# New orders of the pieces in the engine lists of both attentions of a two-layer hybrid encoder

## The reference

```python
def block(q_start, qn, qp):                      # MLA
    sc = (einsum('bqhd,bkhd->bhqk', qn, k_nope) + einsum('bqhr,bkr->bhqk', qp, k_pe)) * scale
    p = softmax(where(chunk_causal_mask(q_start, s), sc, neg), axis=-1)
    return einsum('bhqk,bkhd->bqhd', p, v)

def block(q_start, qb):                          # differential
    sc = einsum('bqhcd,bkhcd->bchqk', qb, k) * scale
    p = softmax(where(chunk_causal_mask(q_start, s), sc, neg), axis=-1)
    a = p[:, 0] - lam * p[:, 1]
    return einsum('bhqk,bkhd->bqhd', a, v)
# then: o = rmsnorm(o, g_subln) * (1 - lambda_init)
```

## Time and profile before

| | |
|---|---|
| median of 3 runs | 2595.37 us (2592.87 to 2596.51) |
| profiled execution, its own time | 2595.02 us |
| its span, first to last instruction | 2593.2 us |
| mean granted clock of TensorE, as a share of full speed | 0.972 |
| PE busy | 2409.5 us, 93% |
| DVE busy | 1794.5 us, 69% |
| ACT busy | 914.6 us, 35% |
| GpSimd busy | 1494.3 us, 58% |

### The profile page before, as it was taken

The page is one execution under the profiler, slowest core; times in us unless marked ns, Lnnn a source line. Parts: engine busy times, 40 slices in busy tenths (PEclk is TensorE's granted clock), DMA queues, the critical chain, the costliest instruction groups (busy, mean ns, idle before and its releaser), DMA issues.

```text
span 2593.2 us, 31553 instructions
## 1 busy us (share of the span) xinstructions
PE 2409.5 (93%) x11916; PEld 1974.8 (76%) x11916; DVE 1794.5 (69%) x2043; ACT 914.6 (35%) x1553; POOL 1494.3 (58%) x1123
## 2 busy tenths in 40 slices
PE   7899999999999999996899899978999999999993
PEld 5688888778888888883677787766778888888882
DVE  3566674797777777778666677763687777777778
ACT  3344442352222222224346565652342222222222
POOL 2222113637999999974441323213628999999982
PEclk9999999999999999997999999988999999999996
DMA  4121225311111111113121212142411111111103
GB/s 155 57 66 63 68 79 198 138 57 57 49 49 49 49 59 64 49 65 126 54 66 33 73 50 90 33 163 107 138 64 42 65 50 49 49 49 59 64 33 130
DMA packets 51237, 191.98 MB, mean 74 GB/s; under 512 B 5904, under 2 KB 6416, under 8 KB 47376
## 3 DMA queue, kind: packets, MB, share of 16 engines
q1 hardware_dynamic: 39184, 148.92, 17.0%
q10 hardware_dynamic: 11904, 41.05, 4.1%
HBM read 146.43 MB, written 29.36 MB: 68 GB/s over the span
## 4 chain that ended last, share of the span: by engine, by line
PE 74%; DVE 15%; ACT 5%; issue 3%; DMA 2%; SPq 1%; ACTq 0%; POOL 0%; POOLq 0%; DVEq 0%
PE ps L1222 9%; PE ps L1224 9%; PE ps L1223 9%; PE ps L1249 6%; PE ps L1251 6%; PE ps L1250 6%; PE ps L1058 3%; PE ps L1030 2%; PE ps L1032 2%; PE ps L1031 2%; PE ps L1095 2%; PE ps L1075 2%; PE ps L1150 1%; PE ps L1015 1%; PE ps L1151 1%
## 5 line engine op out<-in xcount | busy, mean ns | idle before, releaser
L2096 DVE TENSOR_TENSOR a<-a,ps 128x1024 f32<-128x1024 f32 x336 | 408.7, 1217 | 205.9 <-PE ps L1251 194.0
L768 POOL CAST w_hi<-w_raw 128x1024 fp32r<-128x1024 f32 x78 | 85.5, 1096 | 799.9 <-PE ps L1032 276.6
L1249 PE MATMUL ps<-hid,ring 128*128 128x512 f32 x704 | 277.5, 394 | 18.8 <-DVE a L2096 15.3
L850 POOL TENSOR_TENSOR ring<-w_raw,ring 128x512 fp32r<-128x512 f32 x206 | 268.4, 1303 | 16.5
L1250 PE MATMUL ps<-hid,ring 128*128 128x512 f32 x704 | 275.5, 391 | 0.0
L1251 PE MATMUL ps<-hid,ring 128*128 128x512 f32 x704 | 275.4, 391 | 0.0
L1599 ACT ACTIVATE cy<-cx,cv 128x1024 f32<-128x1024 f32 x76 | 94.8, 1247 | 416.7 <-DVE cx L2067 415.4
L1222 PE MATMUL ps<-h,ring 128*128 128x512 f32 x608 | 236.5, 389 | 0.0
L1223 PE MATMUL ps<-h,ring 128*128 128x512 f32 x608 | 236.5, 389 | 0.0
L1224 PE MATMUL ps<-h,ring 128*128 128x512 f32 x608 | 236.5, 389 | 0.0
L848 POOL CAST ring<-w_raw 128x512 fp32r<-128x512 f32 x206 | 128.5, 624 | 122.0 <-PE ps L1177 53.4
(11 more groups left out here) (274 smaller groups left out, 6760.6 us busy)
## 6 DMA issues: line engine op xcount, KB each, us to landing
w_raw<-in_W SPq DMA_DIRECT2D x166, 512.0 KB, 3.2
raw_d<-in_W SPq DMA_DIRECT2D x44, 512.0 KB, 3.8
h<-o_dram ACTq DMA_DIRECT2D x2, 6144.0 KB, 21.4
x_dram<-x ACTq DMA_DIRECT2D x6, 2048.0 KB, 7.2
x<-x_dram SPq DMA_DIRECT2D x2, 4096.0 KB, 12.2
dsw<-draw SPq DMA_DIRECT2D x64, 128.0 KB, 2.3
o_dram<-most SPq DMA_DIRECT2D x6, 1024.0 KB, 4.9
o_dram<-dost SPq DMA_DIRECT2D x6, 1024.0 KB, 4.4
```

Source lines behind the costliest of these rows:

```text
L850: pool.tensor_tensor(lo, raw[name], hi.bitcast(F32), ALU.subtract).then_inc(item_ready, 1)
L1249: pe.matmul(out, wh, xh, start=True, stop=False)
L2096: dve.tensor_tensor(a[:, f, :], a[:, f, :], src, ALU.add).then_inc(acc_done, 1)
```

## The change

The strings of `ORDERS` are replaced, for both attentions and for all four engines. Each new string has the same pieces as the old one, each once; only their order differs. Nothing else in the file is touched; the places, counts, banks, the last chunk that uses a buffer and `load_after` are worked out from the lists as before. Cut to the lines that are spoken of:

```diff
+++ after.py
@@ -164,112 +164,107 @@
...
 ORDERS = {
     "mla": {
         "pe": """
-            E00 E01 Q00 Q01 K00 K01 S000 V00 S001 S010 S011 V01 T000 S020 T010 V02 T011 P000 S021 V03 P010 P011
-            S030 K10 T020 T021 S031 K11 T022 P020 P021 Q10 T030 P022 T031 Q11 P030 T032 P031 K20 P032 T033 S100
-            S101 K21 P033 S110 T100 Q20 P100 S111 Q21 S120 E10 T110 T111 S121 E11 P110 P111 S130 V10 T120 T121
...
-            T232 Q31 P230 P231 T233 K40 P232 P233 S300 K41 S301 S310 S311 Q40 T300 S320 Q41 P300 T310 T311 S321
...
-            Q60 P500 S511 Q61 S520 E30 T510 S521 E31 P510 T511 S530 V30 P511 S531 T520 T521 T522 P520 P521 T530
...
-            P611 V33 S621 K70 S630 T620 K71 T621 P620 T622 S631 Q70 P621 P622 T630 T631 Q71 T632 T633 P630 P631
...
-            P721 T730 P722 T731 T732 P730 P731 T733 P732 P733""",
+            E00 E01 Q00 Q01 K00 K01 V00 S000 S001 K10 S010 S011 T000 V01 S020 P000 Q10 S021 T010 T011 V02 S030 Q11
+            T020 T021 P010 P011 V03 S031 K11 T022 P020 P021 Q20 S100 T030 T031 P022 E10 P030 T032 S101 E11 P031 T033
...
+            T122 S201 Q31 P120 P121 T130 K31 P122 S210 T131 P130 T132 V10 P131 S211 T133 V11 P132 S220 T200 V12 P133
...
+            P420 E30 P421 P422 T430 T431 E31 S510 S511 T432 T433 P430 P431 K61 P432 P433 T500 Q60 S520 Q61 P500 S521
+            S530 T510 T511 S531 Q70 S600 P510 P511 T520 T521 Q71 S601 P520 T522 P521 T530 K70 P522 S610 T531 T532
...
+            V32 S700 S701 T622 P620 P621 S710 S711 T630 P622 T631 V33 T632 T633 P630 P631 S720 T700 S721 P632 P633
+            S730 T710 P700 T711 S731 T720 P710 P711 T721 T722 P720 P721 T730 P722 T731 T732 P730 P731 T733 P732 P733""",
         "act": """
...
+            T610 T611 S621 K71 S630 S631 o61 T620 T621 V32 S700 S701 T622 T630 o62 T631 V33 S710 T632 T633 S711 S720
+            T700 o63 S721 T710 o70 T711 S730 T720 o71 T721 S731 T722 T730 o72 T731 T732 T733 o73""",
...
         "dve": """
...
+            M720 T700 o63 S721 S730 M721 T710 o70 T711 M730 S731 T720 o71 T721 M731 T722 T730 o72 T731 T732 T733 o73""",
         "sp": """
-            L2 L3 WE0 X0 L4 X1 L5 L6 L7 D0 L8 WE1 L9 X2 X3 D1 L10 L11 D2 L12 WE2 L13 X4 X5 D3 L14 L15 D4 WE3 X6
-            X7 D5""",
+            WE0 L2 L3 X0 L4 L5 X1 L6 WE1 L7 D0 L8 X2 X3 D1 L9 L10 L11 WE2 D2 X4 D3 L12 X5 L13 WE3 L14 D4 L15 X6 X7
+            D5""",
     },
...
     "diff": {
         "pe": """
...
-            K71 N61 P620 T621 T622 Q70 P621 P622 T630 T631 Q71 N62 P630 P631 T632 T633 P632 P633 N63 S700 S701
-            S710 S711 T700 P700 S720 N70 T710 T711 S721 P710 P711 N71 S730 T720 T721 P720 P721 S731 T722 P722
-            N72 T730 T731 T732 P730 T733 P731 P732 P733 N73""",
...
+            N53 S621 T610 P600 K70 S630 T611 K71 S631 N60 P610 Q70 P611 T620 T621 Q71 T622 P620 P621 T630 P622 N61
+            T631 P630 N62 S700 S701 T632 P631 T633 S710 S711 T700 P632 S720 P633 S721 T710 N63 P700 S730 T711 P710
+            N70 P711 S731 T720 T721 T722 P720 N71 P721 P722 T730 T731 T732 P730 P731 T733 P732 P733 N72 N73""",
         "act": """
...
-            M630 K70 o61 n60 S631 s60 M631 K71 n61 T621 T622 s61 rK7 Q70 o62 T630 T631 Q71 n62 s62 T632 T633 o63
-            rQ7 n63 s63 S700 S701 M700 M701 S710 T700 S711 M710 o70 M711 n70 S720 s70 T710 T711 M720 o71 S721
-            n71 M721 s71 T720 T721 S730 M730 T722 S731 o72 M731 n72 T730 T731 s72 T732 T733 o73 n73 s73""",
...
+            T630 s60 o62 n61 rQ7 s61 T631 n62 S700 S701 M700 T632 M701 S710 S711 M710 s62 T633 M711 T700 S720 o63
+            M720 T710 S721 n63 o70 M721 T711 s63 S730 o71 n70 M730 T720 T721 S731 T722 M731 s70 n71 T730 T731 o72
+            s71 T732 T733 o73 n72 n73 s72 s73""",
         "dve": """
...
-            T630 T631 Q71 n62 s62 T632 T633 RQ7 rQ7 n63 s63 S700 S701 i700 i701 M700 S710 M701 S711 T700 i710
-            i711 M710 S720 M711 n70 i720 s70 T710 T711 S721 M720 i721 n71 M721 s71 S730 T720 T721 i730 M730 S731
-            T722 i731 M731 n72 T730 T731 s72 T732 T733 n73 s73""",
...
+            T621 M630 M631 n60 Q71 s60 T622 RQ7 T630 n61 rQ7 T631 S700 S701 i700 n62 S710 i701 M700 S711 M701 T632
+            i710 i711 M710 S720 M711 T633 s61 i720 S721 s62 T700 T710 M720 i721 n63 S730 T711 M721 s63 i730 S731 n70
+            T720 M730 i731 T721 T722 M731 s70 n71 T730 T731 T732 T733 s71 n72 n73 s72 s73""",
         "sp": """
-            L2 L3 WK0 L4 WQ0 L5 L6 L7 WK1 L8 WQ1 L9 WK2 L10 WQ2 L11 D0 L12 D1 L13 WK3 L14 WQ3 L15 WK4 D2 L16 WQ4
-            L17 L18 D3 L19 WK5 L20 WQ5 L21 WK6 L22 D4 WQ6 L23 D5 WK7 WQ7 D6""",
+            L2 L3 WK0 WQ0 L4 L5 L6 WK1 L7 WQ1 L8 L9 L10 WK2 D0 WQ2 L11 D1 WK3 L12 L13 WQ3 L14 WK4 L15 WQ4 L16 D2 L17
+            WK5 L18 L19 D3 WQ5 WK6 L20 L21 D4 WQ6 L22 L23 WK7 D5 WQ7 D6""",
     },
 }
...
```

More of the change, by code:

```diff
@@ L177 @@
-            S600 S601 P522 T531 T532 S610 P530 P531 T533 S611 V31 P532 P533 T600 T610 V32 P600 T611 S620 P610
-            P611 V33 S621 K70 S630 T620 K71 T621 P620 T622 S631 Q70 P621 P622 T630 T631 Q71 T632 T633 P630 P631
-            S700 S701 P632 P633 S710 T700 S711 S720 P700 S721 T710 T711 S730 P710 P711 S731 T720 T721 T722 P720
-            P721 T730 P722 T731 T732 P730 P731 T733 P732 P733""",
-        "act": """
[L182 to L193, removed]
@@ L194 @@
-        "dve": """
[L195 to L209, removed]
@@ L215 @@
         "pe": """
[L216 to L220, removed]
@@ L226 @@
-            P511 S530 N51 V30 S531 T520 T521 P520 T522 P521 S600 S601 P522 S610 T530 N52 S611 T531 T532 P530
-            T533 P531 T600 V31 T610 S620 P532 P533 V32 S621 N53 V33 S630 T611 T620 P600 P610 K70 S631 P611 N60
-            K71 N61 P620 T621 T622 Q70 P621 P622 T630 T631 Q71 N62 P630 P631 T632 T633 P632 P633 N63 S700 S701
-            S710 S711 T700 P700 S720 N70 T710 T711 S721 P710 P711 N71 S730 T720 T721 P720 P721 S731 T722 P722
-            N72 T730 T731 T732 P730 T733 P731 P732 P733 N73""",
@@ new lines @@
+            K00 K01 Q00 Q01 V00 S000 S001 V01 S010 S011 V02 S020 T000 V03 P000 T010 S021 N00 K10 T011 S030 K11 S031
+            P010 P011 T020 Q10 P020 T021 T022 Q11 P021 N01 T030 P022 T031 K20 T032 T033 P030 P031 S100 S101 K21 S110
+            S111 P032 P033 N02 T100 S120 Q20 S121 N03 P100 T110 T111 S130 Q21 S131 P110 N10 P111 T120 T121 V10 T122
+            P120 N11 S200 S201 P121 P122 T130 T131 S210 T132 P130 P131 T133 S211 V11 T200 P132 S220 V12 S221 P133
+            V13 N12 N13 T210 P200 S230 K30 T211 N20 K31 T220 S231 P210 T221 P211 Q30 P220 T222 Q31 P221 T230 P222
@@ new lines @@
+            T231 K40 N21 P230 P231 T232 T233 S300 S301 K41 S310 S311 N22 P232 P233 T300 S320 Q40 N23 P300 S321 T310
+            T311 Q41 S330 N30 P310 P311 T320 T321 S331 V20 S400 N31 P320 T322 S401 P321 T330 S410 P322 T331 S411
+            P330 T332 P331 T333 V21 P332 T400 S420 V22 P333 S421 V23 N32 S430 N33 P400 T410 T411 K50 S431 K51 N40
+            P410 P411 T420 T421 Q50 T422 N41 P420 Q51 P421 T430 P422 T431 K60 P430 T432 P431 T433 S500 S501 K61 S510
+            S511 T500 P432 Q60 S520 P433 P500 N42 N43 S521 T510 T511 Q61 S530 P510 N50 P511 T520 S531 T521 V30 S600
```

100 lines of the change are left out of this document (59 added, 41 removed).

## The result

The changed kernel took 2575.47 us (median of 4 runs, 2571.65 to 2577.93), the kernel before beside it 2595.76 (4 runs, 2592.87 to 2596.51): a ratio of 0.9919 [0.9907, 0.9931], or 20 us less. The forecast was 40. The profiled execution took 2573.36 us.

What follows compares the result with a forecast made beforehand. TensorE was taken to bound the kernel, waiting for latency rather than throughput. MLA body 12, differential body 20 and head 7 8 summed to 40 us, so 2595 - 40 = 2555 us; range 2531 to 2584.

Steps and rivals of the forecast that it cites:

- half the gain: Rival, 2576 us: middle pieces on DVE and ACT late for other reasons; MLA 7, body 10, head 7 2; chance 0.2.
- that rival: Rival, slower, 2601 us: DVE standing at the 20 exchanges holds PE 2.3 us each, 46 against 40; chance 0.07.
- MLA body, 12: MLA attention's body: shorter waits of PE and less clock loss save 12 us, bounds 4 and 18.
- the two terms for waits: MLA body: 6 of the 8.0 us behind DVE's block tails go, and the 2.8 before one chunk.
- the term of 3 for clock and hidden pauses: MLA body: fewer pauses give back 3 us of lower-clock time and short pauses hidden in the rows.
- MLA opening, 0: Start of the MLA attention: PE's order hardly changes, so 0, between -2 and +2 us.
- Differential body, 20: Differential attention's body: shorter waits of PE, clock and hidden pauses save 20 us, bounds 6 and 32.
- The terms for P (8.5) and N (3.5): Differential body: probabilities-times-V waits shrink 6.5 behind DVE and 2 behind the previous output; norm-sum waits shrink 3.5 of 4.7.
- The terms for S and T (2.5): Differential body: waits of score pieces and transposes shrink by 2.5 us.
- Last score piece of a block to its first T: Both attentions: median PE work before the first transpose grows, MLA 6.2 to 11.2 us, differential 11.7 to 14.3.
- Head 7, 8: Last differential head: a serial score chain with two shortened links saves 8 us, bounds 0 and 16.
- The two shortened links: Head 7: one exponent no longer behind an output copy; work from last scores to their transposes grows 1.3 to 3.6 us.

Runs made afterwards that it cites:

- the doubling: All 20 exchanges of halves done twice, the second after the first landed: 2674.59 us on the changed kernel, 2710.63 us on the kernel before.
- the part that was tested: GpSimd's multiplications by the norm gains left out of the differential attention: 2564.82 us on the changed kernel, 2585.48 us on the kernel before.
- the last kernel: Changed kernel with transposed-block tails ahead of norms and rotations in all differential heads, plus the MLA opening's old nine-piece order on ACT and DVE: 2592.99 us.

## Why the prediction was half right

The measured 2575.5 us lie in the stated range, but 9 us above the favoured forecast of 2543 to 2566: the range held because it took in the rival "half the gain", which had a chance of 0.2.

- **Direction and mechanism** were right: PE waited for latency, and longer distances in its list took those waits away. P behind DVE fell to 0.5 us in the differential body (under 4 forecast) and to 0.4 in MLA (under 2). The feed-forward parts stayed equal, and the bulk load cost nothing, as worked out. The exchange did not take over the end: DVE's wait there stayed at 18.6 and 18.4 us, so that rival fell.
- **MLA body, 12:** measured 15 (311.1 to 298.9, with the 2.9 us of the opening set apart), inside the bounds of 4 and 18. The size is right, its make-up less so: 6.5 us of idle time went, not the 8.8 of the two terms for waits, and the term of 3 for clock and hidden pauses came out at 8 to 9. Of this the clock is worth up to 5.7 (283 us at 0.98, now 1.00).
- **MLA opening, 0:** it cost 2.9 us in this profile, 1.0 to 3.2 in the six kernels with these MLA lists, two of them outside the 2 allowed; the lower clock there (0.76 for 0.88) goes with it. The prediction named V00 ahead and RE0 later on DVE and priced both at nothing. That rE00 meets a split is new, but the old places on ACT and DVE don't bring the time back.
- **Splits on GpSimd, 0:** waits of PE behind a split are new, 1.4 us in each body.
- **Differential body, 20:** 7.9 us less idle time, about 10 by the windows (434 to 424). The terms for P (8.5) and N (3.5) were, if anything, small: 11.3 and 4.7. The terms for S and T (2.5) and for the chunks (2) had the wrong sign: -6.4 and -1.8. The clock term of 3.5 did not come: 0.99 in both. The failed step is "Last score piece of a block to its first T": it counted the work on PE's list between the two, 11.7 and now 14.3 us, and took more as a gain. It left out that the maximum, the scaling and the chunk tails each have a place on DVE's list, where they came later too.

The two traces show this block by block. The table gives means over heads 0 to 6 (28 blocks of each attention, 70 pairs of T and P), in us, worked out from the rows of every piece:

| | MLA before | MLA after | differential before | differential after |
|---|---|---|---|---|
| last product of the scores to first product of T | 5.7 | 10.1 | 12.1 | 16.2 |
| of it until the second M has ended | 3.4 | 6.8 | 8.1 | 12.2 |
| left over | 2.4 | 3.3 | 4.0 | 4.0 |
| first T within 0.3 us of that M's end | 4 | 2 | 4 | 7 |
| last product of T to first product of P | 3.4 | 5.1 | 7.5 | 9.1 |
| of it until the low part is written | 1.8 | 2.9 | 2.8 | 5.0 |
| left over | 1.6 | 2.1 | 4.8 | 4.1 |
| P within 0.3 us of that low part's end | 11 | 0 | 9 | 3 |

PE's distances grew as planned, and the tightest pairs of T and P are gone. But in the differential attention the probabilities became ready 4.1 us later, as much as the distance to T had grown, so nothing was left over for T, and 7 blocks in place of 4 have their T right behind M. It is not the step from the maximum to the exponent (0.8 us before, 0.7 after) but the one from the exponent to the scaling M: 2.5 us before, 6.9 after. In DVE's list 12 of the 56 M pieces of these heads stood behind a chunk's step that comes after their own scores' maximum, now 43; behind the maximum of a later block 10, now 26. So it is with block 2 of head 3 (timelines of 1485:1492 in the changed kernel and of 1503.5:1508 in the one before); M321 is the row of 128x768:

```profile
1485.84 0.69 DVE L1840 TENSOR_TENSOR dt<-ps,dcos 128x512 f32<-128x512 f32 x1 [2.46 <-ACT draw L1406]
1486.76 2.02 DVE L1894 TENSOR_REDUCE nb<-ps 128x2 f32<-128x1792 f32 x1 [0.23 <-PE ps L1070]
1488.70 1.01 DVE L1914 SCALAR_TENSOR_TENSOR dprob<-dprob,rec,dprob 128x768 f32<-128x768 f32 x1
...
1489.86 1.06 PE L1090 MATMUL ps<-ident,dprob 128*128 128x128 f32 x8 [1.16 <-DVE dprob L1914]
```

```profile
1504.00 1.02 DVE L1919 SCALAR_TENSOR_TENSOR dprob<-dprob,rec,dprob 128x768 f32<-128x768 f32 x1 [0.24 <-ACT dprob L1482]
1505.58 0.69 DVE L1845 TENSOR_TENSOR dt<-ps,dcos 128x512 f32<-128x512 f32 x1 [0.56 <-ACT draw L1411]
1506.50 2.02 DVE L1899 TENSOR_REDUCE nb<-ps 128x2 f32<-128x1792 f32 x1 [0.23 <-PE ps L1075]
```

The new list puts Q41 and S330 ahead of M321, and T320 waits for it. The prediction held that late pieces are rarer in both new bodies; T pieces right behind their M are more frequent in the differential one. That the places on DVE and ACT can cost as much as the change gave is shown by the kernel with the tails ahead in all heads, and that the way through the exchange has little more room than before by the doubling. No run moves M ahead of the chunks and the next maxima with PE's list kept, so how much of the 10 us or so that are missing this would give is not shown.

- **Head 7, 8:** 0 (idle time 20.0 and 20.2 us, windows of 63 and 64 us where 55 were to be expected). The two shortened links were real, yet the chain kept its length: the wait moved from S, M and N to T and P behind DVE. The rival "half the gain" had named that place, T631 behind rQ7. Two kernels that moved those tails gained nothing or lost 7 to 10 us. The prediction had also left out a wait that was there before: P behind DVE, 5.8 us, beside the 4.8 and 4.7 that it named. The 1 us for one more norm at the way out was looked for at N72; what the chain shows is s70 and n71 ahead of T730's tail, 3.66 us with the meeting, where n72 alone stood before (0.48).
- **The rival "half the gain, 2576"** gave the time that came, from the mechanism it named: late middle pieces on DVE. Its sizes were off: MLA gave more than its 7 (12.2), the body 8 to 10 of its 10, head 7 none of its 2. Of its second cause, the meeting with GpSimd, the part that was tested costs 8 us in both orders.

## What to carry to other kernels

Where several engines each run a fixed list, a gap in the bounding engine's list is worth only what the middle pieces' places on the other lists allow. Count for every moved piece what now stands ahead of it on each engine, and add up the losers beside the winners. To learn whether a step has slack, double it under both orders and compare the growth in each stage, with the granted clock of each beside it: here it fell from 0.95 to 0.88 with the longer waits, and part of the growth was its doing. To see whether a longer distance was worth anything, take from the trace what was left over between the middle piece's end and its consumer, before and after. And a wait that a reordering removes from one link of a serial chain is not a gain until the next link has been looked at.

## What the runs showed of the hardware

- A 64x1024 operation with a scalar and a tensor operand took 1.22 us alone and 3.28 where GpSimd's subtraction of 2.35 us had begun 0.14 earlier; in the seven kernels with that order it took 3.27 or 3.28. The sum 1.22 + 2.21 (what was left of the subtraction) is 3.43. The Trainium skill ("SBUF — State Buffer", Who interferes with whom) has the later one wait until the first has ended; the rows agree to within 0.15 us.
- An exchange of 2.41 us from issue, done twice, cost 5.5 to 6.0 us each in the differential attention, in both orders, with the granted clock of that stage down from 0.95 to 0.88.
- Runs of one and the same kernel can spread by more than 10 us: the eleven of the last kernel took 2582.72 to 2594.49 us. Its profiled execution was the fastest of them, with 541.3 us in the differential attention; the kernel with the same differential lists, profiled at 2594.5, its median, showed 550.9. So a stage's time in one profile has to be read beside that execution's place among the kernel's runs.
